# Norms 2 and 3 by token sums, eight plain block products for the first feed-forward pair, and the last down group by token halves

## Chip, core and metric

The kernel runs on one core of one Trainium2 chip. The metric is the device time of one execution in microseconds (us); the kernel before takes 1563.1 us (median of 3 runs, 1559.49 to 1563.49).

## What is computed

One encoder block on x of 1024 tokens by 1024 features, float32. The parts that the change touches, cut from the reference:

```python
def rms_norm(x, g):
    xf = x.astype(jnp.float32)
    y = xf * lax.rsqrt(jnp.mean(xf * xf, axis=-1, keepdims=True) + NORM_EPS)
    return (y * g.astype(jnp.float32)).astype(x.dtype)
...
        x = x + jnp.concatenate([o_rwkv, o_att], axis=-1) @ w_out[l]
        h = rms_norm(x, ln2_g[l])                                        # norm 2
        gate = depthwise_conv_centred(h @ ffn_w_gate[l], ffn_conv_w[l], ffn_conv_b[l])
        x = x + (jax.nn.gelu(gate, approximate=False) * (h @ ffn_w_up[l])) @ ffn_w_down[l]
    return rms_norm(x, lnf_g)                                            # norm 3
```

h is 1024 x 1024, the gate and up weights 1024 x 2816, the down weights 2816 x 1024.

## The kernel before

Everything is kept transposed: features on the 128 partitions in 8 tiles (k = 0 to 7), tokens on the free axis. Precise products are made of three matmuls in a faster float32 format, high x high, high x low and low x high; for this each operand is split: ScalarE copies the high part (names with `hi`), VectorE or GpSimd subtracts it for the low part (`lo`). A semaphore counts each such step.

A norm before (`norm`, L603 to 605; `norm_root`, L908; `rstd`, L1340; `normalised`, L1346) runs so: ScalarE squares each finished tile of x, VectorE adds the squares into `acc` [128 x 1024]; TensorE multiplies `acc` by a matrix of ones, which gives the sum of every token on all 128 partitions; ScalarE takes the root of [128 x 1024]; VectorE takes the reciprocal of [128 x 1024] into `rs`; eight products x * gain * `rs` follow. Norm 2 stands between the output projection and the feed-forward part, norm 3 ends the program.

The gate and up weights are taken in 22 pairs of column tiles (f = 0 to 21). For a pair, [gate; up] times the 2 x 2 blocks of h (B11, B12, B21, B22: feature half, token half) is made with seven block products instead of eight (`PRODUCTS`, `pair_products`, L857): operands `op` 0 to 6 are B11, t1 = B12 - B11, t2 = B22 - t1, B21, B22 - B12, B22 and B21 - t2 (x_sum, L1625, splits by `operand_hi` and `operand_lo`); weight sums are made on GpSimd (`weight_sums`, L1297 to 1302). One block product is 12 matmuls of 512 columns. Each product waits for its operand (`h_lo`), for its weights (`w_lo`), and some for an eviction of an earlier bank (`v_out`, `comb`). Pairs 0 and 1 run first, since their operands are being made meanwhile; the other 20 run in a loop. Beside pair f, ScalarE and VectorE split the weights of pair f + 1 (`pair_hi`, `pair_lo`), combine, convolve, apply GELU and multiply; the gated result goes to DRAM.

The down projection takes the 22 tiles of the gated result in groups of 8, 8 and 6. In a group each of the 8 output tiles (m) is one unit: its weights are loaded (`load_down`), split, multiplied over all 1024 tokens, and VectorE adds the result to x. In the last group a unit is 6 x 3 x 2 = 36 matmuls; ScalarE and VectorE square and sum each finished tile, so that norm 3 starts after the last one.

All engines run their own lists in the order written; only the semaphores tie them.

## Time and profile before

| | us |
|---|---|
| median of 3 runs | 1563.1 |
| the profiled execution, its own time | 1563.26 |
| its span | 1561.4 |
| output projection ends, norm 2 begins | 824 |
| first gate/up product begins | 852.36 |
| pairs run without a gap from | 884.60 |
| last matmul of the down projection ends | 1533.4 |

Of the page, these lines matter first (engine, busy us, share of the span, instructions; then forty slices of the span, with the granted TensorE clock in tenths):

```profile
PE 1411.1 (90%) x10892; PEld 1036.2 (66%) x10892; DVE 882.8 (57%) x1095; ACT 567.3 (36%) x812; POOL 182.2 (12%) x146
...
PE   6889898979899899987893699999999998999993
...
PEclk9999999989989999898996899999999999999997
```

PE is TensorE's matmuls and PEld its weight loads, DVE is VectorE, ACT is ScalarE, POOL is GpSimd, SP issues the DMAs. Each digit is a slice of 39 us. TensorE is the busiest engine and is close to full in slices 24 to 39; it is low in slices 22 and 23 (norm 2 and the first pair) and in the last one (norm 3 and the stores).

### The profile page before, as it was taken

The numbers are of one execution on the slowest core, as the hardware profiler recorded it, in microseconds if no ns is written. First come the engines' busy times: TensorE is split into PE (matmuls) and PEld (weight loads), VectorE is DVE, ScalarE is ACT, GpSimd is POOL, SyncE is SP. The second block draws the span as 40 slices with busy tenths as digits, with TensorE's granted clock in tenths as the row PEclk, the third lists the DMA queues.
The fourth block names the chain that finished last, engine by engine and source line by source line (L and its number), as shares of the span: only waits on it lengthen the run. The fifth ranks groups of instructions, "written<-read, shape, count | busy, mean of one in ns | idle before, by whom it ended". The sixth has DMA issues, their size and how long they took to land. (4 is left out here: it accounts for less than half of the span.)

```text
span 1561.4 us, 27687 instructions
## 1 busy us (share of the span) xinstructions
PE 1411.1 (90%) x10892; PEld 1036.2 (66%) x10892; DVE 882.8 (57%) x1095; ACT 567.3 (36%) x812; POOL 182.2 (12%) x146
## 2 busy tenths in 40 slices
PE   6889898979899899987893699999999998999993
PEld 3354545454477687765782588888888887888882
DVE  5664563759456567675437855555555563332235
ACT  3424141411146566666212544333334442121121
POOL 0110000101001000003034022222222200000000
PEclk9999999989989999898996899999999999999997
DMA  5036557385636657541141022222222236322112
GB/s 201 31 87 146 121 125 168 83 181 153 171 113 220 202 159 234 162 136 58 41 161 41 18 88 87 89 82 81 81 81 81 81 137 253 107 81 91 40 30 107
DMA packets 168439, 179.86 MB, mean 115 GB/s; under 512 B 76784, under 2 KB 132208, under 8 KB 168272
## 3 DMA queue, kind: packets, MB, share of 16 engines
q1 hardware_dynamic: 158800, 163.22, 35.3%
q0 software_dynamic: 2880, 9.83, 2.0%
q10 hardware_dynamic: 6720, 6.29, 1.3%
q8 instruction: 23, 0.38, 0.1%
q14 instruction: 16, 0.13, 0.0%
HBM read 121.76 MB, written 57.54 MB: 115 GB/s over the span
## 5 line engine op out<-in xcount | busy, mean ns | idle before, releaser
L872 PE MATMUL banks<-op,sw_hi 128*128 128x512 f32 x1232 | 381.8, 391 | 32.8 <-DVE op L1327 30.4
L872 PEld LDWEIGHTS banks<-op,sw_hi 128*128 128x128 f32 x1232 | 232.6, 189 | 83.5 <-issue 35.4
L576 PE MATMUL banks<-hT,work 128*128 128x512 f32 x576 | 255.1, 603 | 18.3 <-DVE hT L1386 6.4
L872 PE MATMUL banks<-op,sw_lo 128*128 128x512 f32 x616 | 240.6, 391 | 0.0
L576 PEld LDWEIGHTS banks<-hT,work 128*128 128x128 f32 x576 | 110.5, 193 | 159.9 <-issue 146.6
L1608 DVE TENSOR_TENSOR xT<-xT,banks 128x1024 f32<-128x1024 f32 x32 | 39.1, 1221 | 210.7 <-PE banks L588 199.1
L872 PEld LDWEIGHTS banks<-op,sw_lo 128*128 128x128 f32 x616 | 116.3, 189 | 24.3
L1124 ACT ACTIVATE sw_hi<-work 128x1024 fp32r<-128x1024 f32 (+1 forms) x66 | 78.9, 1200 | 96.1 <-PE banks L872 94.7
L588 PE MATMUL banks<-g_hi,down_hi 128*128 128x512 f32 x352 | 109.5, 392 | 4.0 <-DVE g_lo L1327 4.0
L1327 DVE TENSOR_TENSOR sw_lo<-work,sw_hi 128x1024 fp32r<-128x1024 f32 (+1 forms) x63 | 88.0, 1398 | 39.8 <-ACT sw_hi L1124 39.7
L588 PE MATMUL banks<-g_lo,down_hi 128*128 128x512 f32 x352 | 109.2, 392 | 0.0
L588 PE MATMUL banks<-g_hi,down_lo 128*128 128x512 f32 x352 | 109.0, 391 | 0.0
L1086 ACT ACTIVATE down_hi<-work 128x1024 fp32r<-128x1024 f32 (+1 forms) x24 | 23.6, 988 | 176.4 <-PE banks L588 176.4
L588 PEld LDWEIGHTS banks<-g_hi,down_hi 128*128 128x128 f32 x352 | 66.5, 189 | 18.2 <-DVE g_lo L1327 4.4
L588 PEld LDWEIGHTS banks<-g_lo,down_hi 128*128 128x128 f32 x352 | 66.6, 189 | 14.0
L588 PEld LDWEIGHTS banks<-g_hi,down_lo 128*128 128x128 f32 x352 | 66.6, 189 | 13.9
L1297 POOL TENSOR_TENSOR work<-work 128x512 f32<-128x512 f32 x22 | 29.0, 1317 | 346.1 <-DMA work<-in_w_gu 346.1
L1164 ACT ACTIVATE hT<-banks,par 128x1024 f32<-128x1024 f32 x22 | 24.6, 1118 | 115.8 <-DVE banks L1662 115.8
L1397 DVE SCALAR_TENSOR_TENSOR work<-banks,par,work 128x1023 f32<-128x1023 f32 x12 | 15.4, 1280 | 82.4 <-ACT work L932 82.4
L745 PE MATMUL banks<-work 32*64 32x64 f32 x1024 | 40.0, 232 | 15.1 <-DMA work<-TI_d 5.1
L745 PEld LDWEIGHTS banks<-work 32*64 32x64 f32 x1024 | 35.4, 143 | 20.3 <-ACT work L1074 9.9
L588 PE MATMUL banks<-h_hi,w_hi 128*128 128x512 f32 x128 | 41.0, 402 | 6.1 <-DVE h_lo L1327 3.0
(187 smaller groups left out, 2184.7 us busy)
## 6 DMA issues: line engine op xcount, KB each, us to landing
work<-scan_d SPq DMA_DIRECT2D x32, 768.0 KB, 4.9
work<-in_w_gu SPq DMA_DIRECT2D x88, 256.0 KB, 4.0
scan_d<-work SPq DMA_DIRECT2D x16, 1024.0 KB, 6.0
g_d<-hT SPq DMA_DIRECT2D x22, 512.0 KB, 3.0
work<-in_w_in SPq DMA_DIRECT2D x20, 512.0 KB, 3.8
scan_d<-work SPq DMA_DIRECT2D x32, 256.0 KB, 6.2
work<-in_w_down SPq DMA_DIRECT2D x16, 512.0 KB, 3.9
work<-g_d SPq DMA_DIRECT2D x15, 512.0 KB, 4.6
```

Source lines behind the costliest of these rows:

```text
L576: mm = pe.matmul(out[:, h * HALF:(h + 1) * HALF], wt[:, k, :], src[:, k, h * HALF:(h + 1) * HALF], start=(k == 0), stop=(k == kn - 1))
L588: mm = pe.matmul(out[:, h * HALF:(h + 1) * HALF], wp[slot][:, k, :], xp[k][:, h * HALF:(h + 1) * HALF], start=(opens and k == (ks or range ...
L745: pe.matmul(XY[z][64 * e:64 * e + 64, j * HD:(j + 1) * HD], Gs[slot][hk, z, j, c2 * 64:c2 * 64 + 64], UV[slot][hk, z, c2, j, :], start=(j ...
L872: mm = pe.matmul(banks[:, 3 * slot + bank, :], w[:, n, k * P:(k + 1) * P], x[n][:, k, :], start=(opens and k == 0 and p_ == 0), stop=(k == ...
L1086: act.activation(dst[slot][:, 0:kn, :], raw[slot][:, 0:kn], ACT.Copy).then_inc(wt["hi"][slot], 1)
L1124: act.activation(sw_hi[:, lo_:hi_, :], wsrc[slot][:, lo_:hi_], ACT.Copy).then_inc(fs["w_hi"], 1)
L1164: act.activation(ga[slot], flat[:, 3 * slot * HALF:(3 * slot + 2) * HALF], ACT.Copy, scale=col("cw1", f))\
L1297: pool.tensor_tensor(x[:, 1], x[:, 7], x[:, 6], ALU.add).then_inc(fs["sums"], 1)
L1327: tt(out, x, hi.bitcast(F32), ALU.subtract).then_inc(done, 1)
L1397: stt(dst[:, 1:T], ps[slot][:, 0:T - 1], col("mu_prev", m), dst[:, 1:T], ALU.mult, ALU.add)\
L1608: tt(x, x, product, ALU.add).then_inc(added[slot], 1)
```

## The change

Norms 2 and 3 in compact form: `token_norm` makes the sum of each token with one column of ones, so that tokens stand on partitions and the sums of 1024 tokens are [128 x 8]; root and reciprocal act on that; `spread` multiplies a broadcast column by the identity, which puts the values back on all partitions as [128 x 1024] in PSUM (`rms_rows`), where `normalised` reads them.

The first pair: the eight plain block products (4 weight blocks x 2 token halves), whose operands need no sums; its 4 weight blocks are split in [128 x 512] pieces by ScalarE and VectorE. The operand sums and the remaining splits move behind its start, pair 1 stays with seven products but waits for each operand by `H_NEEDED`, and the steps of pair 0 (convolution, GELU, gating) are written out between them. GpSimd no longer makes sums or low parts for pair 0, and starts the sums of pair 2 once all operands are split.

The last down group: all 8 output tiles for tokens 0 to 511, then all 8 for tokens 512 to 1023. The 8 tiles' weights are loaded in the first half and kept for the second. In the second half norm 3 of the first half's tokens runs, with its two TensorE steps behind units 1 and 2, and its 8 outputs are stored (SP); after the last unit the norm of the other half follows.

The diff, cut to its core:

```diff
-H_FIRST = 3
+PLAIN = ((0, 0, 0), (1, 0, 2), (0, 1, 1), (1, 1, 6), (2, 2, 0), (2, 3, 1), (3, 2, 2), (3, 3, 6))
+H_NEEDED = (3, 7, 8, 5, 9, 6, 10)
...
+            def token_norm(count, ts_=range(NT)):
+
+                pe.wait_ge(ns["summed"], count)
+                for t in ts_:
+                    mm = pe.matmul(token_sums[:, t:t + 1], acc[:, t * P:(t + 1) * P], ones[:, 0:1], start=True, stop=True)
+                mm.then_inc(ns["ms_mm"], 1)
+            def spread(n, ts_=range(NT)):
+
+                pe.wait_ge(ns["rstd"], n + 1)
+                for t in ts_:
+                    mm = pe.matmul(rms_rows[:, t * P:(t + 1) * P], token_rms[:, t:t + 1].broadcast_to([P, P]), ident[:, :],
+                                   start=True, stop=True)
+                mm.then_inc(ns["ms_mm"], 1)
...
-            norm(1, acc)
+            token_norm(2 * (KD - 1))
+            spread(1)
+            def eight_products():
+
+                x_at = (0, 4, 3, 5)
+                for n, (w_at, x, bank) in enumerate(PLAIN):
+                    if n in (0, 1, 4):
+                        pe.wait_ge(fs["w_lo"], (1, 2, 0, 0, 3)[n])
+                    if n in (0, 2, 4, 5):
+                        pe.wait_ge(sp_s["h_lo"], (3, 0, 4, 0, 5, 6)[n])
+                    for k in range(4):
+                        for p_, (w, x_) in enumerate(((sw_hi, op_hi), (sw_hi, op_lo), (sw_lo, op_hi))):
+                            mm = pe.matmul(banks[:, bank, :], w[:, w_at, k * P:(k + 1) * P], x_[x_at[x]][:, k, :],
+                                           start=(n < 4 and k == 0 and p_ == 0), stop=(k == 3 and p_ == 2),
+                                           skip_group_check=True)
+                    if n % 2:
+                        mm.then_inc(fs["prod"], 4 if n == 7 else 1)
...
-                    if first and slot == 0:
-                        pe.wait_ge(sp_s["h_lo"], H_FIRST + n)
+                    if first:
+                        pe.wait_ge(sp_s["h_lo"], H_NEEDED[n])
...
+            eight_products()
+            pair_products(1, 1, True)
+            pe.wait_ge(fs["x_sums"], 7)
...
+            f0, fn = GROUPS[-1]
+            n0 = down_unit(len(GROUPS) - 1)
+            for h in range(2):
+                for m in range(KD):
+                    i, slot = m // 2, m % 2
+                    if h == 0:
+                        pe.wait_ge(wt["lo"][slot], n0 + i + 1 + FREE)
+                    pe.wait_ge(added[slot], n0 + 4 * h + max(i - 1, -h) + FREE)
+                    for k in range(fn):
+                        if h == 0 and m == 0:
+                            pe.wait_ge(fs["g_lo"], f0 + k + 1)
+                        g = g_place(f0 + k)
+                        for p_, (w, x) in enumerate(((last_hi, g_hi), (last_hi, g_lo), (last_lo, g_hi))):
+                            mm = pe.matmul(banks[:, 6 * slot + i % 2, :], w[m][:, k, :], x[g][:, token_half[h]],
+                                           start=(k == 0 and p_ == 0), stop=(k == fn - 1 and p_ == 2))
+                    mm.then_inc(wt["used"][slot], 1)
+                    if h == 1 and m == 1:
+                        token_norm(3 * (KD - 1), range(4))
+                    if h == 1 and m == 2:
+                        spread(2, range(4))
+            token_norm(4 * (KD - 1), range(4, NT))
+            spread(3, range(4, NT))
...
+            def norm_root(n, ts_=slice(0, NT)):
+
+                act.wait_ge(ns["ms_mm"], 2 * n if n else 1)
+                out, sums = (token_rms[:, ts_], token_sums[:, ts_]) if n else (rs, ps[2])
+                act.activation(out, sums, ACT.Sqrt, bias=eps[:, 0:1], scale=1.0 / D).then_inc(ns["root"], 1)
...
+            act.wait_ge(src_full[0], 64)
+            for w_at, b in ((0, 0), (1, 7), (2, 3), (3, 6)):
+                w = act.activation(sw_hi[:, w_at, :], wsrc[0][:, b], ACT.Copy)
+                if w_at != 2:
+                    w.then_inc(fs["w_hi"], 1)
             norm_root(1)
...
             operand_hi(0, B11)
+            operand_hi(4, B12)
+            act.wait_ge(ns["scaled"], 2 * KD)
+            operand_hi(3, B21)
+            act.wait_ge(s["out_stored"], 16 * KD)
+            operand_hi(5, B22)
+            pair_hi(1, 1, 0)
             act.wait_ge(fs["x_sums"], 1)
             operand_hi(1, t1)
             act.wait_ge(fs["x_sums"], 2)
-            act.wait_ge(sp_s["h_lo"], 4)
+            act.wait_ge(sp_s["h_lo"], 7)
             operand_hi(2, t2)
-            act.wait_ge(ns["scaled"], 2 * KD)
-            operand_hi(3, B21)
-            act.wait_ge(fs["prod"], 1)
-            act.activation(V, banks[:, 0, :], ACT.Copy).then_inc(fs["v_out"], 1)
             act.wait_ge(fs["x_sums"], 3)
-            operand_hi(4, B12)
-            act.wait_ge(s["out_stored"], 16 * KD)
-            operand_hi(5, B22)
-            act.wait_ge(fs["x_sums"], 4)
-            operand_hi(6, B21)
+            act.wait_ge(fs["prod"], 3)
+            act.activation(ga[0], ps[0], ACT.Copy, scale=col("cw1", 0)).then_inc(fs["scaled"], 1)
+            pair_hi(1, 1, 1)
+            operand_hi(4, B22)
...
+            act.sem_inc(fs["v_out"], 1)
+            act.wait_ge(fs["prod"], NPROD + 1)
+            act.activation(V, banks[:, 3, :], ACT.Copy).then_inc(fs["v_out"], 1)
+            pair_hi(1, 1, 2)
+            act.wait_ge(fs["x_sums"], 5)
+            act.activation(ga[0], ga[0], ACT.Gelu, bias=col("cb", 0)).then_inc(fs["gelu"], 1)
+            act.wait_ge(fs["x_sums"], 6)
+            operand_hi(6, B21)
...
+            def last_weights_hi(m):
+
+                if m >= 2:
+                    for slot in range(2):
+                        act.wait_ge(wt["used"][slot], down_unit(len(GROUPS) - 1) + FREE)
+                act.wait_ge(wt["full"][m % 2], 16 * (down_unit(len(GROUPS) - 1) + m // 2) + 16)
+                act.activation(last_hi[m][:, 0:LAST_N, :], down_raw[m % 2][:, 0:LAST_N], ACT.Copy).then_inc(wt["hi"][m % 2], 1)
+
+            def square_half(h, k):
+
+                act.wait_ge(added[k % 2], down_unit(len(GROUPS) - 1) + KD // 2 * h + k // 2 + 1 + FREE)
+                if k >= 3:
+                    act.wait_ge(ns["summed"], (2 + h) * (KD - 1) + k - 2)
+                out = acc if k == 0 else sqb[k % 2]
+                act.activation(out[:, token_half[h]], xT[:, k, token_half[h]], ACT.Square).then_inc(ns["squared"], 1)
...
+            norm_root(2, slice(0, 4))
+            for k in range(KD):
+                square_half(1, k)
+            norm_root(3, slice(4, NT))
...
-            for slot in range(2):
-                weight_sums(slot, slot, 64)
-            for g, (lo_, hi_) in enumerate(((0, 2), (2, 4), (4, 7))):
-                pool.wait_ge(fs["w_hi"], g + 1)
-                pool.tensor_tensor(sw_lo[:, lo_:hi_, :], wsrc[0][:, lo_:hi_], sw_hi[:, lo_:hi_, :].bitcast(F32), ALU.subtract)\
-                    .then_inc(fs["w_lo"], 1)
+            weight_sums(1, 1, 64)
+            pool.wait_ge(sp_s["h_lo"], 10)
...
+            def rstd(n, ts_=slice(0, NT)):
 
                 dve.wait_ge(ns["root"], n + 1)
-                dve.reciprocal(rs, rs).then_inc(ns["rstd"], 1)
-                dve.wait_ge(ns["rstd"], n + 1)
+                dve.reciprocal(token_rms[:, ts_], token_rms[:, ts_]).then_inc(ns["rstd"], 1)
+                dve.wait_ge(ns["ms_mm"], 2 * n + 1)
...
-                    stt(hT[:, k, :], xT[:, k, :], col(gain, k), rs, ALU.mult, ALU.mult).then_inc(ns["scaled"], 1)
+                    stt(hT[:, k, :], xT[:, k, :], col(gain, k), rms_rows, ALU.mult, ALU.mult).then_inc(ns["scaled"], 1)
...
+            for w_at, b in ((0, 0), (1, 7), (2, 3), (3, 6)):
+                dve.wait_ge(fs["w_hi"], (1, 2, 3, 3)[w_at])
+                w = tt(sw_lo[:, w_at, :], wsrc[0][:, b], sw_hi[:, w_at, :].bitcast(F32), ALU.subtract)
+                if w_at != 2:
+                    w.then_inc(fs["w_lo"], 1)
+            dve.sem_inc(fs["comb"], 8)
...
             normalised("ln2", range(4))
             dve.wait_ge(ns["scaled"], KD + 4)
-            x_sum(t1, B12, B11)
-            operand_lo(0, B11)
-            dve.wait_ge(fs["x_sums"], 1)
-            operand_lo(1, t1)
+            operand_lo(0, B11, 1)
+            operand_lo(4, B12, 2)
             normalised("ln2", range(4, KD))
             dve.wait_ge(ns["scaled"], 2 * KD)
+            operand_lo(3, B21, 3)
+            operand_lo(5, B22, 4)
+            x_sum(t1, B12, B11)
+            dve.wait_ge(fs["x_sums"], 1)
+            dve.wait_ge(fs["prod"], 2)
             x_sum(t2, B22, t1)
-            x_sum(B12, B22, B12)
             dve.wait_ge(fs["x_sums"], 2)
-            operand_lo(2, t2)
-            operand_lo(3, B21)
+            dve.wait_ge(sp_s["h_lo"], 6)
+            x_sum(B22, B22, B12)
...
-            dve.wait_ge(sp_s["h_lo"], 6)
+            pair_lo(1, 1, 0)
+            operand_lo(1, t1, 5)
+            operand_lo(2, t2, 6)
+            pair_lo(1, 1, 1)
+            dve.wait_ge(fs["scaled"], 1)
+            g, gate = ga[0], ps[0]
+            stt(g[:, 1:T], gate[:, 0:T - 1], col("cw0", 0), g[:, 1:T], ALU.mult, ALU.add).then_inc(fs["x_sums"], 1)
+            dve.wait_ge(fs["x_sums"], 4)
+            stt(g[:, 0:T - 1], gate[:, 1:T], col("cw2", 0), g[:, 0:T - 1], ALU.mult, ALU.add).then_inc(fs["x_sums"], 1)
+            early_sum(1, 1, 0)
+            dve.wait_ge(sp_s["h_lo"], 8)
             x_sum(B21, B21, t2)
-            early_sums(0, 0)
-            dve.wait_ge(fs["x_sums"], 4)
-            operand_lo(4, B12)
-            operand_lo(5, B22)
-            operand_lo(6, B21)
-            dve.wait_ge(fs["w_lo"], 3)
-            dve.wait_ge(sp_s["h_lo"], H_FIRST + NPROD - 1)
-            pair_lo(1, 1, 0)
-            rest_of_pair(0, 0)
-            early_sums(1, 1)
+            dve.wait_ge(fs["x_sums"], 6)
+            operand_lo(4, B22, 7)
+            pair_lo(1, 1, 2)
+            early_sum(1, 1, 1)
+            operand_lo(6, B21, 8)
+            dve.wait_ge(fs["gelu"], 1)
+            for h, bank in enumerate((2, 6)):
+                dve.wait_ge(fs["prod"], NPROD)
+                half = ga[0][:, h * HALF:(h + 1) * HALF]
+                gated_half = tt(half, half, banks[:, bank, :], ALU.mult)
+            gated_half.then_inc(fs["x_sums"], 1)
+            dve.wait_ge(sp_s["h_lo"], 10)
             pair_lo(2, 0, 0)
...
+            for m in range(KD):
+                add_half(0, m)
+                if m < KD - 2:
+                    low_part(last_lo[m + 2][:, 0:LAST_N, :], down_raw[m % 2][:, 0:LAST_N], last_hi[m + 2][:, 0:LAST_N, :],
+                             wt["hi"][m % 2], down_unit(len(GROUPS) - 1) + m // 2 + 2, wt["lo"][m % 2])
+                if m >= 2:
+                    add_square_half(0, m - 1)
+            add_square_half(0, KD - 1)
+            for m in range(KD):
+                add_half(1, m)
+                if m >= 2:
+                    add_square_half(1, m - 1)
+                if m == 2:
+                    rstd(2, slice(0, 4))
+                if m >= 3:
+                    normalised_half(0, range(2 * m - 6, 2 * m - 4) if m < 7 else ())
+            add_square_half(1, KD - 1)
+            rstd(3, slice(4, NT))
+            normalised_half(1, range(KD))
```

## Rows read from the trace of the kernel before

**Rows 1.** Stages: stretch, its us, each engine's busy us (instructions), clock, DMA.
```profile
824.00:852.00 28.00, 3.87 (x6) 1.18 (x4) 22.59 (x10) 9.25 (x7) 11.75 (x5) 0.63 0.16 56
852.00:887.00 35.00, 22.47 (x83) 17.51 (x84) 32.90 (x20) 14.12 (x10) 6.87 (x3) 0.81 0.00 1
1468.00:1534.00 66.00, 65.40 (x289) 53.83 (x287) 22.09 (x21) 13.36 (x14) 0.00 (x0) 1.00 0.11 30
1534.00:1561.40 27.40, 2.98 (x4) 0.82 (x4) 19.23 (x12) 3.45 (x3) 0.00 (x0) 0.57 0.39 153
```

**Rows 2.** Chain of waits in time: start us, us, what ran.
```profile
884.60 402.84 PE banks L872 x1776
```

**Rows 3.** TensorE timeline, norm 2 to pair 1: start, us, [idle before].
```profile
828.10 3.64 PE L599 MATMUL banks<-bonusT,ones 128*128 128x512 f32 x4 [3.87 <-DVE bonusT L1338]
...
852.36 1.19 PE L872 MATMUL banks<-op,sw_hi 128*128 128x512 f32 x2 [20.62 <-DVE op L1327]
...
869.22 1.19 PE L872 MATMUL banks<-op,sw_hi 128*128 128x512 f32 x2 [9.74 <-DVE op L1327]
...
877.10 0.47 PE L872 MATMUL banks<-op,sw_hi 128*128 128x512 f32 x1 [0.66 <-issue]
```

**Rows 4.** VectorE timeline, same stretch.
```profile
825.40 2.55 DVE L1338 TENSOR_TENSOR bonusT<-bonusT 128x1024 f32<-128x1024 f32 x2
...
832.92 6.55 DVE L1343 RECIPROCAL bonusT<-bonusT 128x1024 f32<-128x1024 f32 x1 [4.97 <-ACT bonusT L911]
...
839.51 3.51 DVE L1349 SCALAR_TENSOR_TENSOR hT<-xT,par,bonusT 128x1024 f32<-128x1024 f32 x1
...
848.85 3.36 DVE L1327 TENSOR_TENSOR op<-hT,op 128x2048 fp32r<-128x2048 f32 x1
...
866.79 2.29 DVE L1327 TENSOR_TENSOR op<-bonusT,op 128x2048 fp32r<-128x2048 f32 x1
```

**Rows 5.** ScalarE and GpSimd timelines, same stretch.
```profile
831.78 1.11 ACT L911 ACTIVATE bonusT<-banks,c_eps 128x1024 f32<-128x1024 f32 x1 [5.20 <-PE banks L599]
...
846.64 1.91 ACT L1133 ACTIVATE op<-hT 128x2048 fp32r<-128x2048 f32 x1 [10.49 <-DVE hT L1349]
...
850.14 3.20 POOL L1299 TENSOR_TENSOR work<-work 128x512 f32<-128x512 f32 x1
```

**Rows 6.** Groups by shape: line, operation xcount | busy us, mean ns.
```profile
L1124 ACT ACTIVATE sw_hi<-work 128x1024 fp32r<-128x1024 f32 x44 | 46.3, 1056 | 81.1 <-PE banks L872 81.0
...
L1327 DVE TENSOR_TENSOR sw_lo<-work,sw_hi 128x1024 fp32r<-128x1024 f32 x42 | 51.3, 1223 | 39.8 <-ACT sw_hi L1124 39.7
...
L1650 DVE TENSOR_TENSOR hT<-hT,banks 128x512 f32<-128x512 f32 x44 | 30.0, 684 | 19.8 <-PE banks L872 19.8
...
L1297 POOL TENSOR_TENSOR work<-work 128x512 f32<-128x512 f32 x22 | 29.0, 1317 | 346.1 <-DMA work<-in_w_gu 346.1
...
L1006 ACT ACTIVATE work<-work,c_eps 128x8 f32<-128x8 f32 x8 | 2.0, 292 | 0.0
...
L1513 DVE RECIPROCAL work<-work 128x4 f32<-128x4 f32 x16 | 2.9, 178 | 0.6
```

**Rows 7.** TensorE timeline: eight 128-column float32 operations, and two gaps.
```profile
736.77 1.03 PE L827 MATMUL banks<-ident,hT 128*128 128x128 f32 x8
...
744.19 0.74 PE L588 MATMUL banks<-h_hi,w_hi 128*128 128x512 f32 x2 [1.40 <-POOL h_lo L1290]
...
1300.92 1.22 PE L588 MATMUL banks<-g_hi,down_hi 128*128 128x512 f32 x2 [3.98 <-DVE g_lo L1327]
```

**Rows 8.** VectorE timeline of the tail, after the last matmul.
```profile
1533.44 1.22 DVE L1608 TENSOR_TENSOR xT<-xT,banks 128x1024 f32<-128x1024 f32 x1 [5.80 <-PE banks L588]
...
1541.43 6.55 DVE L1343 RECIPROCAL bonusT<-bonusT 128x1024 f32<-128x1024 f32 x1 [4.31 <-ACT bonusT L911]
...
1548.02 9.66 DVE L1349 SCALAR_TENSOR_TENSOR hT<-xT,par,bonusT 128x1024 f32<-128x1024 f32 x8
```

**Rows 9.** DMA issues: x count, KB each, us to landing.
```profile
work<-in_w_down SPq DMA_DIRECT2D x8, 384.0 KB, 3.1
```

143 lines of the change are left out of this document (83 added, 60 removed).

## Prediction

> **What bounds the kernel now.** I read the stages first [rows 1]. Between 907 and 1290 us and in the down projection TensorE has no gap: the chain of waits has 1776 matmuls in one piece of 402.84 us [rows 2], 0.2268 us each, so a block product of 12 costs 2.72 us and one of the last group's units of 36 costs 8.16 us. No part of the change shortens that. What is left is in three places. From 824 to 852 us TensorE is busy 3.87 of 28.00 us; from 852 to 887 it is busy 22.47 of 35.00 us; from 1534 to the end it is busy 2.98 of 27.40 us [rows 1]. In the TensorE timeline the reader is to see who ends the gaps [rows 3]: norm 2's sum starts at 828.10, the first product at 852.36 when VectorE has split B11, then come gaps of 9.74 us (again a VectorE split) and 0.66 us; the piece of rows 2 starts at 884.60, with the seventh product of pair 0. Pair 1 so ends at 884.60 + 8 x 2.72 = 906.4 us. VectorE is the limit in both norm stretches (32.90 of 35.00 us busy [rows 1]), and one half of its load is plain size: a reciprocal of 6.55 us, sums and splits of 2048 elements at 2.29 us, 2.21 start to start [rows 4].
>
> All sums below are against the profiled execution, 1563.26 us (span 1561.4 and 1.9 around it); it lies 0.16 us above the median, so I take its number as the median's.
>
> **Part 1, norm 2.** Unchanged up to the last add of squares, which ends at 827.95 [rows 4]. Before, 11.56 us pass until the first normalised tile starts at 839.51 [rows 4]: sum 3.64 [rows 3], root 1.11 [rows 5], reciprocal 6.55 and handovers. After: `token_norm` is 8 float32 matmuls of one column. Nothing like it stands in the trace. The nearest row is eight 128-column operations, 1.03 us in all, and since the last lasts 0.27, 0.109 us start to start at the full clock [rows 7]. A float32 matmul is two records (rows 3 has 4 for the two of the old sum), so 16 records: 1.7 us at 2.4 GHz, 3.4 at 1.2 GHz. TensorE has idled 3.87 us before it, and the old sum took 0.85 us a record there, with a mean granted clock of 0.63 in the stretch [rows 1, 3]; I take 3.4, and 0.35 for start and drain. The root on [128 x 8] is 0.29, the reciprocal of [128 x 4] 0.18 [rows 6], for 8 columns 0.2, each with 0.05 for the handover. `spread` is 8 matmuls of 128 columns, again 16 records: 1.7 or 3.4 us; 3.4 and 0.2, as nothing dense ran before it. Sum 7.9, less the bounds 4.5 (both at full clock) and 11 (0.3 a record). So normalising starts at 835.6 instead of 839.5: gain 3.9. Cover: the 4 + 4 weight pieces put ahead of root and reciprocal are 4 x 0.6 on ScalarE (half of 1.06 and a start; behind its last square, which the add at 827.95 has waited for) and 4 x 0.61 on VectorE (0.68 less the overlap; 827.95 to 830.5) [rows 4, 6], both before the token sums end at 831.7; without that cover they would cost 2.4.
>
> **Part 2, normalising and pairs 0 and 1.** Take 835.6 as zero. The rows show a price that goes away: the first normalising instruction took 3.51 us while GpSimd made low parts, and the split of B11 3.36 instead of 2.29 while it made sums [rows 4, 5]; undisturbed the eight of norm 3 take 9.66 / 8 = 1.2 [rows 8]. GpSimd now has nothing to do here. The SBUF page of the Trainium skill (SBUF — State Buffer, Who interferes with whom) says that only a VectorE instruction with two SBUF inputs contends with GpSimd, and normalising now reads one of them from PSUM; by that rule it would be free of the price even with GpSimd busy, by the rows it is free because GpSimd is idle, and the sum is the same.
>
> VectorE: four tiles to 4.8; ScalarE's high part of B11 (1.91 [rows 5]) to 6.8; low part to 9.1. TensorE starts at 9.2, that is 844.8 instead of 852.36. Eight products are 96 x 0.2268 = 21.8 us. The restart at the lower clock costs what it did before: products 0 and 1 ran from 852.36 to 859.48, 1.5 us over 24 x 0.2268 [rows 3]; I take 1.6. They end at 32.6 if the operands keep up, and they do: low part of B12 at 11.3 (needed 16.3), B21 at 20.4 (needed 21.7), B22 at 22.6 (needed 24.4). The 9.74 us gap is gone; 12 matmuls more (2.7 us) are its price.
>
> Then VectorE's list, at 2.21 a step, is t1 24.8, t2 27.2, B22 - B12 29.5, pair 1's first weights 30.6 (1.15 [rows 6]), low t1 32.9; ScalarE makes the high part of t2 only behind that (34.8), low t2 37.2, second weights 38.3. Pair 1's products 0 and 1 fill 32.6 to 38.0, product 2 waits 0.4, product 3 ends at 43.9. VectorE goes on with two convolution steps (40.9), Q (41.6), B21 - t2 (43.8), low part of B22 - B12 (46.1), third weights (1536 elements, 1.7: 47.8) and U2 (48.4). Product 4 needs all of these: **a new gap of 4.6 us**, and with it 1.6 for the clock, since behind 3.98 us of idling two matmuls took 1.22 us and behind 1.40 us two took 0.74 [rows 7]. Products 4 to 6 end at 58.3. Pair 1 ends at 835.6 + 58.3 = 893.9 instead of 906.4: parts 1 and 2 gain **12.5 us**. GpSimd starts pair 2's sums when the last operand is split (50.7), two are there at 53.3, high and low parts at 55.6, 2.7 before TensorE asks. (Sums are 1.3 each [rows 6].) From there on the loop is the old one.
>
> **Part 3, the last group.** Twice 8 units of 18 matmuls: as many as before. In the first half weights come twice as fast, one set of 384 KB in 4.08 us, landing after 3.1 us [rows 9]. A unit's raw buffer is free 1.9 us after the unit two earlier ends, +3.1 for the load, high part 0.85, and the low part, behind VectorE's next add, is there 2.2 us before its unit. In all, a load may be 4.5 us late before TensorE waits; I charge nothing. Per unit VectorE has 0.68 + 0.95 + 0.68 and ScalarE 0.85 + 0.6 of 4.08 (0.95 and 0.85 are halfway between the times for 512 and 1024 columns [rows 6]).
>
> In the second half two steps stand in TensorE's stream. Token sums of 4 columns: 8 records, 0.9. `spread` behind unit 2 waits for the reciprocal, which VectorE's list has behind the add of unit 2 itself (0.2 + 0.68), a square's add (0.6) and 0.18: TensorE idles 1.8 us, too little for the clock [rows 7], then 0.9. Cost **3.6 us** (bounds 1.8, the wait hidden, and 5.5).
>
> After the last matmul, before: 1561.4 - 1533.4 = 28.0, of which 9.66 normalising, 6.55 reciprocal, 3.7 from the last tile to the end [rows 8]. After: add 0.7, square 0.65, add 0.7 (512 columns, [rows 6]), token sums of 4 columns 1.2, root 0.3, reciprocal 0.2, spread 0.9 to 1.8 and 0.3 around it, eight half tiles at 0.67 (1.2 less 512 / 1024 of 1.07) 5.4, stores 3.7: 14.6. Gain 13.4, net **9.8**.
>
> Code: the last group's 288 matmuls are now written out instead of looped. The page Runtime: NRT & Kernel Launch (Instruction fetch mechanics) of the Trainium skill says that sequential fetch is hidden and taken branches may stall; by it the written-out code costs 0. The straight code of pair 0 has one gap of 0.66 us that no semaphore explains [rows 3]. Three more of those would be 2 us; zero is in the sum, 2 in the range.
>
> **Sum.** 1563.3 - 12.5 - 9.8 = **1541.0 us**. Own range 1535.5 to 1546.5: norm 2 -3.4 to +3.1, the clock behind the new gap 0 to 2.3, part 3 -1.8 to +1.9, code +2, not all at one end.
>
> **Rivals.**
> (a) GpSimd's late start becomes the new wait. Against VectorE splits its sums took 3.20 us instead of 1.3 [rows 5], VectorE 3.36 for 2.29. If all four do, the second pair of sums is ready at 61.4 instead of 55.9, pair 2's first weights at 59 and its second at 64: TensorE loses 1 to 2, and VectorE's late work runs into pair 2's evictions for as much again. With a norm 2 at its long bound: 1546.5 to 1552. For it: nothing hides the sums but 2.7 us. Against: VectorE's gating reads PSUM.
> (b) Small matmuls and the spread run at full clock, the clock holds through the new gap: 1531 to 1535.5.
> (c) The halves bring nothing: unit by unit the weights come 1 us late (5 units) and the two inserted steps cost 8. The tail gains about 1: 1548 to 1553.
> (d) Slower: the weight supply of the first half decides. The point is a landing of 7.6 us (3.1 + 4.5); beyond it each of the 6 late units waits for the excess. To end above 1568 it must eat 22 + 5 us, 4.5 a unit, a landing of 12 us: 1568 to 1580. For it: the load rate doubles to 96 GB/s and every load is asked for only when its buffer is free. Against: the DMA share is 0.11 in that stretch [rows 1], 0.22 when doubled.
> (e) It doesn't do what it says: the compact root and reciprocal cost as much as the big ones, by handovers, and the operands keep VectorE as late as before: within 5 us of 1563.
>
> **Chances.** Forecast 0.68, (b) 0.10, (a) 0.11, (c) 0.04, (d) 0.04, (e) 0.03. The range 1534 to 1549 takes in the forecast, half of (b) and most of (a). About 0.3% (4.7 us) is what a measurement of this kernel can tell from no change. Faster by more: 0.93; within: 0.03; slower: 0.04.
>
> **What the profile after would show.** First gate/up product near 845, eight products without a gap, one gap of 4 to 5 us before pair 1's fifth product, ended by VectorE's U2 (L1650 before), then one piece to the down projection. GpSimd silent all through norm 2 and pair 0, until about 886. In the last half-group one idle of 1.8 us behind the third unit, and 14 to 15 us from the last matmul to the end. The forecast is wrong if a float32 matmul of one column costs over 0.6 us, if TensorE waits for `last_lo` weights, or if pair 2 starts with a wait for GpSimd's sums.

## The result, and the profile after

| | before | after |
|---|---|---|
| median of the runs made together | 1561.3 us (1557.5 to 1563.49) | 1543.5 us (1541.41 to 1550.63) |
| ratio of the times, 95% interval | 1 | 0.9889 [0.9844, 0.9933] |
| profiled execution (its span) | 1563.26 us (1561.4) | 1550.63 us (1548.8) |
| mean granted TensorE clock | 0.953 | 0.955 |

The change makes the kernel 1.1% faster, some 17.8 us, where 22.3 were forecast; 1543.5 lies within 1534 to 1549. One later execution of the kernel before took 2931.81 us, nearly twice as long as all others, and stands in no ratio. The profiled execution of after is the longest of its four and only 12.6 us below that of before, so the first reading is where the difference of the two spans lies. The stages, chosen to answer rows 1 (columns as there: stretch, its us, busy us of TensorE, its weight loads, VectorE, ScalarE, GpSimd, then the granted clock and the DMA share):

```profile
830.80:852.00 21.20, 7.56 (x34) 6.97 (x32) 13.28 (x14) 7.11 (x8) 0.00 (x0) 0.58 0.21 75
852.00:903.00 51.00, 45.64 (x180) 36.83 (x181) 42.95 (x29) 21.82 (x16) 8.66 (x6) 0.91 0.09 31
1470.00:1534.50 64.50, 63.03 (x285) 51.85 (x283) 27.97 (x42) 14.53 (x22) 0.00 (x0) 1.00 0.18 59
1534.50:1548.80 14.30, 3.55 (x17) 3.12 (x16) 7.52 (x12) 0.89 (x2) 0.00 (x0) 0.60 0.41 152
```

Counted from an event that both kernels have, the end of norm 2's last add of squares (827.95 before [rows 4], 834.76 after):

| stretch, us | before | after | difference |
|---|---|---|---|
| start to the last add of squares (code unchanged) | 828.0 | 834.8 | +6.8 |
| to the first normalised tile | 11.56 | 8.10 | -3.5 |
| from there to the first block product | 12.85 | 9.34 | -3.5 |
| from there to the end of pair 1 | 54.1 | 50.9 | -3.2 |
| to the last matmul of the down projection | 627.0 | 631.5 | +4.5 |
| to the end | 28.0 | 14.3 | -13.8 |

The first line isn't the change's. Between these two executions 6.4 of the 6.8 us arise from 455 to 525 us, in the first steps of the scan; over the profiles below the same event lies anywhere from 825.2 to 835.8 us, in kernels whose code is the same up to there. Without it the profiled execution would be 1543.8. The lines under it are steady to some tenths from one profile to the next, so the parts are sized by them, and the whole by the medians.

TensorE after, in the two stretches (start us, us, tiles, count, [idle before and what ended it]):

```profile
834.91 3.54 PE L632 MATMUL banks<-ones,bonusT 128*128 128x1 f32 x16 [3.87 <-DVE bonusT L1441]
...
839.04 3.78 PE L639 MATMUL banks<-ident,work 128*128 128x128 f32 x16 [0.59 <-DVE work L1446]
...
852.20 1.20 PE L900 MATMUL banks<-op,sw_hi 128*128 128x512 f32 x2 [9.38 <-DVE op L1430]
...
891.29 0.70 PE L921 MATMUL banks<-op,sw_hi 128*128 128x512 f32 x2 [3.48 <-DVE hT L1761]
...
900.30 0.70 PE L921 MATMUL banks<-op,sw_hi 128*128 128x512 f32 x2 [1.69 <-DVE hT L1772]
```

VectorE, then GpSimd, in the same time:

```profile
838.79 0.20 DVE L1446 RECIPROCAL work<-work 128x8 f32<-128x8 f32 x1 [1.62 <-ACT work L982]
...
842.86 4.86 DVE L1452 SCALAR_TENSOR_TENSOR hT<-xT,par,banks 128x1024 f32<-128x1024 f32 x4 [3.88 <-PE banks L639]
...
890.46 0.68 DVE L1761 TENSOR_TENSOR hT<-hT,banks 128x512 f32<-128x512 f32 x1
...
896.07 3.48 DVE L1430 TENSOR_TENSOR sw_lo<-work,sw_hi 128x1024 fp32r<-128x1024 f32 x2 [1.53 <-ACT sw_hi L1201]
...
899.48 0.67 DVE L1772 TENSOR_TENSOR hT<-hT,banks 128x512 f32<-128x512 f32 x1
```

```profile
893.59 1.28 POOL L1404 TENSOR_TENSOR work<-work 128x512 f32<-128x512 f32 x1 [86.63 <-DVE op L1430]
...
896.20 2.27 POOL L1407 TENSOR_TENSOR work<-work 128x512 f32<-128x512 f32 x1
```

Most of the forecast signs are there. The sums of norm 2 are 16 records of one column and take 3.54 us, its reciprocal 0.20 instead of 6.55 [rows 4]. The first product is at 852.20, 9.34 us behind the first normalised tile, since the four tiles take 4.86 us and none of them 3.51 [rows 4]. There is no gap for 35.6 us, then one of 3.48 us, ended by U2 (L1761); product 4 of pair 1 starts 48.43 us from the first tile. GpSimd is silent for 86.63 us. The last row of the TensorE fence was not forecast: 1.69 us before pair 1's last product, ended by `up_second` (L1772). The two splits ahead of that add (896.07) take 3.48 us beside GpSimd's sums of 2.27 us; in the kernel before two such splits met no sums and took 2.36:

```profile
881.49 2.36 DVE L1327 TENSOR_TENSOR sw_lo<-work,sw_hi 128x1024 fp32r<-128x1024 f32 x2
```

So 1.1 of these 1.69 us are again VectorE and GpSimd meeting. From pair 1's last product on the chain of waits has one piece, as before [rows 2]:

```profile
900.30 383.80 PE banks L921 x1692
```

The last group's second half and the tail (TensorE, then VectorE):

```profile
1506.28 0.95 PE L632 MATMUL banks<-ones,bonusT 128*128 128x1 f32 x8
...
1512.94 1.16 PE L639 MATMUL banks<-ident,work 128*128 128x128 f32 x8 [1.47 <-DVE work L1446]
...
1536.72 1.43 PE L632 MATMUL banks<-ones,bonusT 128*128 128x1 f32 x8 [2.18 <-DVE bonusT L1893]
...
1538.71 2.08 PE L639 MATMUL banks<-ident,work 128*128 128x128 f32 x8 [0.56 <-DVE work L1446]
```

```profile
1538.48 0.18 DVE L1446 RECIPROCAL work<-work 128x4 f32<-128x4 f32 x1 [1.81 <-ACT work L982]
...
1540.83 5.36 DVE L1899 SCALAR_TENSOR_TENSOR hT<-xT,par,banks 128x512 f32<-128x512 f32 x8 [2.17 <-PE banks L639]
```

Sums (0.95 us) and spread (1.16 us, behind 1.47 us of idle time) stand in the second half's stream; unit 1 to unit 2 takes 5.03 us and unit 2 to unit 3 6.82, where the others take 4.08: 3.7 us in all, at full clock (the stretch to 1534.5 has 1.00). Behind the last matmul the reciprocal of 6.55 us is one of 0.18 (rows 8 against this fence) and normalising takes 5.36 instead of 9.66. The written-out code of the 288 matmuls shows no gap but the 1.47 us in front of the spread. By the page Runtime: NRT & Kernel Launch (Instruction fetch mechanics) of the Trainium skill, sequential fetch is hidden; the trace agrees (no such gap in the 69 us from 1465.6 to 1534.5).

### The profile page after: what moved, and what is told of

Its sections match the earlier page's. It is cut to its first block, busy times and chain, and to the rows that moved or that the text cites. A ratio compares the mean times of both kernels' runs of the same rounds, so it can differ in the third digit from the quotient of the medians.

```text
span 1548.8 us, 27771 instructions
## 1 busy us (share of the span) xinstructions
PE 1426.1 (92%) x10960; PEld 1053.1 (68%) x10960; DVE 866.4 (56%) x1120; ACT 544.0 (35%) x803; POOL 164.7 (11%) x139
## 4 chain that ended last, share of the span: by engine, by line
PE 76%; DVE 10%; ACT 5%; DMA 4%; issue 3%; POOL 1%; SPq 1%; ACTq 1%; DVEq 0%; POOLq 0%
PE banks L921 25%; PE banks L593 17%; PE banks L605 15%; PE banks L956 4%; PE banks L777 2%; PE banks L787 2%; PE banks L806 2%; PE banks L616 2%; ACT work L1093 2%; PE banks L758 1%; PE banks L747 1%; PE banks L694 1%; PE banks L821 1%; PE banks L737 1%; DVE op L1430 1%
## 5 line engine op out<-in xcount | busy, mean ns | idle before, releaser
L921 PE MATMUL banks<-op,sw_hi 128*128 128x512 f32 x1176 | 363.8, 391 | 5.2 <-DVE hT L1761 3.5
L921 PEld LDWEIGHTS banks<-op,sw_hi 128*128 128x128 f32 x1176 | 221.3, 188 | 52.0 <-DVE sw_lo L1430 3.9
L921 PE MATMUL banks<-op,sw_lo 128*128 128x512 f32 x588 | 229.5, 390 | 0.0
L1711 DVE TENSOR_TENSOR xT<-xT,banks 128x1024 f32<-128x1024 f32 x24 | 29.3, 1221 | 169.1 <-PE banks L605 157.1
L1430 DVE TENSOR_TENSOR sw_lo<-work,sw_hi 128x1024 fp32r<-128x1024 f32 (+1 forms) x63 | 89.1, 1414 | 39.3 <-ACT sw_hi L1201 39.3
L605 PE MATMUL banks<-g_hi,down_hi 128*128 128x512 f32 x256 | 79.8, 393 | 5.4 <-DVE g_lo L1430 4.8
L605 PE MATMUL banks<-g_lo,down_hi 128*128 128x512 f32 x256 | 79.3, 391 | 0.0
L605 PE MATMUL banks<-g_hi,down_lo 128*128 128x512 f32 x256 | 79.3, 391 | 0.0
L605 PEld LDWEIGHTS banks<-g_hi,down_hi 128*128 128x128 f32 x256 | 48.5, 190 | 16.0 <-DVE g_lo L1430 5.2
L605 PEld LDWEIGHTS banks<-g_lo,down_hi 128*128 128x128 f32 x256 | 48.5, 189 | 10.2
L605 PEld LDWEIGHTS banks<-g_hi,down_lo 128*128 128x128 f32 x256 | 48.4, 189 | 10.0
```

What stands on the lines that cost most here:

```text
L605: mm = pe.matmul(out[:, h * HALF:(h + 1) * HALF], wp[slot][:, k, :], xp[k][:, h * HALF:(h + 1) * HALF], start=(opens and k == (ks or range ...
L921: mm = pe.matmul(banks[:, 3 * slot + bank, :], w[:, n, k * P:(k + 1) * P], x[n][:, k, :], start=(opens and k == 0 and p_ == 0), stop=(k == ...
L1430: tt(out, x, hi.bitcast(F32), ALU.subtract).then_inc(done, 1)
L1711: tt(x, x, product, ALU.add).then_inc(added[slot], 1)
```

## The experiments

For the single parts one source was made in which norms, eight products and halves each have a switch; with all three on it is meant to do what the kernel after does, which has a source of its own. Times are medians beside runs of the kernel before on the same chip (19 runs, 1564.4 us, for the first four below; 1561.4 for the other four). The ratio, taken over the runs, and not the difference of the medians says what a change is worth; the two differ by up to 2.2 us. All stage figures stand in one table behind the experiments.

### The kernel after, again

No edit: the kernel after, beside its parts.

> The changed kernel again, beside the three parts alone. Theory A (the first profile of it ran 6.8 us late before the change's first instruction): its stages are as before, 8.1 us from the last add of squares to the first normalised tile, 60.2 from there to the end of pair 1, 14.3 from the last matmul to the end, and its time is 17 to 21 us below the kernel before. Rival: the late upstream part belongs to the change, and is there again; then it stands 10 to 14 us below.

1548.6 us, ratio 0.9885 [0.9851, 0.9919]. This is the same ratio as in the first comparison (0.9889), at a time 5 us higher, as the kernel before is 3 us higher too. The change is worth 1.1%, 18 us by the ratio (the medians differ by 15.8). In this profile the first gap is 4.26 us and the second 0.54, and pair 1 ends at 60.15 us from the first tile, as at 60.2 above: pair 1's last product starts at 57.43 us (57.44 above) whatever the clock does between the two gaps, since VectorE's list releases it.

### Halves alone

```diff
-NORM2, EIGHT, TAIL = True, True, True
+NORM2, EIGHT, TAIL = False, False, True
```

> The kernel before with part 3 alone (last down group and norm 3 by token halves). Theory A: the parts add, each is worth what its own stage shows: 13.7 us less behind the last matmul, 3.7 us more inside the group, so 10 us less in all (1553 against 1563). Rival (the halves bring nothing because the rest of the chain hides them, or starve for weights): within 2 us of the kernel before, with waits of TensorE on the weights' low parts.

1554.1 us, ratio 0.9935 [0.9903, 0.9967]: 10.2 us of gain (5 to 15 in the interval), where 9.8 were forecast. The tail is 13.23 us instead of 28.04, and the stretch up to pair 1 is as before (78.2 us against 78.5). Part 3 stands alone and was sized right.

### Compact norms alone

Norm 2 and norm 3 (undivided) by token sums, root and reciprocal of [128 x 8] and spread; products and last group as before.

```diff
-NORM2, EIGHT, TAIL = True, True, True
+NORM2, EIGHT, TAIL = True, False, False
```

> The kernel before with both norms in compact form, the last one over all tokens at once, pairs and down group as before. Theory A: norm 2's chain from the last add of squares to the first normalised tile falls from 11.6 to 8.1 us, and behind the last matmul 3 us go (28.0 to 25): 6 to 7 us less in all, up to 2 more since normalising reads one operand from PSUM and so does not meet GpSimd's low parts (3.51 us for its first instruction should become 1.3). Rival (small matmuls and handovers eat what the root and reciprocal give): less than 2 us.

1548.9 us, ratio 0.9887 [0.9855, 0.992]: as much as all three parts together, within the intervals. Its stages show less: 9.3 us up to the end of pair 1 (69.2 against 78.5) and 3.3 in the tail (24.8 against 28.0), 12.6 in all, which the interval of the ratio (12.5 to 22.7 us) just takes in. The stages, not these four runs, size this part. The 9.3 us is more than the 3.5 us that the shorter chain explains. TensorE, VectorE and GpSimd of this kernel:

```profile
852.55 1.19 PE L938 MATMUL banks<-op,sw_hi 128*128 128x512 f32 x2 [9.57 <-DVE op L1515]
...
866.31 1.19 PE L938 MATMUL banks<-op,sw_hi 128*128 128x512 f32 x2 [5.42 <-DVE op L1515]
```

```profile
843.02 4.86 DVE L1542 SCALAR_TENSOR_TENSOR hT<-xT,par,banks 128x1024 f32<-128x1024 f32 x4 [3.88 <-PE banks L651]
...
850.12 2.28 DVE L1515 TENSOR_TENSOR op<-hT,op 128x2048 fp32r<-128x2048 f32 x1
```

```profile
839.93 8.06 POOL L1496 TENSOR_TENSOR sw_lo<-work,sw_hi 128x1024 fp32r<-128x1024 f32 x3 [29.62 <-ACT sw_hi L1235]
```

The four tiles of the kernel before, of which [rows 4] shows the first:

```profile
839.51 7.09 DVE L1349 SCALAR_TENSOR_TENSOR hT<-xT,par,bonusT 128x1024 f32<-128x1024 f32 x4
```

In the norms-only kernel GpSimd still makes low parts of the weights while VectorE normalises, the very meeting that made one normalising step 3.51 us before [rows 4]. Now four take 4.86 us, 1.2 each. What has changed is where VectorE reads the rows of reciprocal roots: `rms_rows` is PSUM, `rs` was SBUF. The gap before product 3 is 5.42 us instead of 9.74 for the same reason: the second four tiles take 4.85 (6.93 before). Not all of it is the operand's place. Of the 3.3 us by which the first product comes nearer to the first tile (9.53 against 12.85) 2.2 are the tiles, and 1.1 are the split of B11, 2.28 us instead of 3.36 [rows 4]. That split reads SBUF alone in both kernels; here GpSimd's sums, which wait for a DMA, start behind it, 10.7 us from the first tile instead of 8.7. So part 1 removes, besides the chain, the meeting that part 2 removes by silencing GpSimd.

### Eight products alone

```diff
-NORM2, EIGHT, TAIL = True, True, True
+NORM2, EIGHT, TAIL = False, True, False
```

With `EIGHT` on, the source puts norm 2's `rs` into free columns of the weights' low parts, as the products' operands take its old place:

```python
        rs1 = rs if not EIGHT else work[:, SW_AT - KD * T + 12 * BK_:SW_AT - KD * T + 14 * BK_]
```

> The kernel before with the eight block products for pair 0 alone (norms and down group as before; the inverse root of norm 2 lies in another place, because an operand needs its old one). Theory A: from the first normalised tile to the end of pair 1 it takes 60 us instead of 66.9, so 6 to 7 us less in all; gap of about 3.5 us before pair 1's fifth product and of about 1.7 before its seventh. Rival (the eight products only pay together with the short norm, since the early list of VectorE is what limits): 0 to 3 us.

1557.7 us, ratio 0.9959 [0.9929, 0.9989], 6.4 us of gain; by stages 7.0 (71.5 against 78.5).

```profile
845.19 4.87 DVE L1542 SCALAR_TENSOR_TENSOR hT<-xT,par,work 128x1024 f32<-128x1024 f32 x4
```

```profile
895.93 1.28 POOL L1481 TENSOR_TENSOR work<-work 128x512 f32<-128x512 f32 x1 [89.87 <-DVE op L1515]
```

The rows of reciprocal roots are in SBUF here, GpSimd is silent, and the four tiles take 4.87 us. For these tiles either remedy gives the whole of it.

### Norms and halves, without the eight products

```diff
-NORM2, EIGHT, TAIL = True, True, True
+NORM2, EIGHT, TAIL = True, False, True
```

> The changed kernel with part 2 undone: compact norms and the halves, but seven products for pair 0 as before. Theory B (after the norms-only run: reading the inverse roots from PSUM takes VectorE out of GpSimd's way, and that gives most of what the eight products give): pair 1 ends 61 us after the first normalised tile, 1 us later than in the changed kernel, so the time stands 18 to 19 below the kernel before. Theory A (parts add): 6.7 us above the changed kernel, 12 below the kernel before.

1545.4 us, ratio 0.9892 [0.9853, 0.9931], against 0.9885 and 0.9889 with them. Pair 1 ends 68.1 us behind the last add of squares, with the eight products 68.3 and 67.8. Its gap before product 3:

```profile
860.98 1.19 PE L938 MATMUL banks<-op,sw_hi 128*128 128x512 f32 x2 [6.16 <-DVE op L1515]
```

The eight products take this gap of 6.16 us away, together with the 2.1 of the two later gaps (0.37 and 1.77), and pay 2.72 us for 12 more matmuls, 3.48 and 1.69 for the new gaps and the clock behind them. On top of compact norms they bring between -0.2 and +0.3 us by these profiles, and 0.9 to 1.4 against the norms alone (69.2), whose code in this stretch is the same as here (68.1). What the eight products add is not clear of the 1.1 us between these two profiles of the same code.

### Rows of reciprocal roots in SBUF

Compact norms alone, but ScalarE copies `rms_rows` to SBUF and norm 2's tiles are scaled from the copy (`token_rms` moves to another tile, since the copy takes its place).

```diff
+                act.wait_ge(ns["ms_mm"], 3)
+                act.activation(rs, rms_rows, ACT.Copy).then_inc(s["kk_chain"], 1)
...
-    stt(hT[:, k, :], xT[:, k, :], col(gain, k), rms_rows, ALU.mult, ALU.mult)
+    stt(hT[:, k, :], xT[:, k, :], col(gain, k), rs if gain == "ln2" else rms_rows, ALU.mult, ALU.mult)
```

> The norms-only kernel with one step more: ScalarE copies the inverse roots of norm 2 from PSUM to SBUF (1.1 us) and normalising reads them there. Theory B (the operand's place decides whether VectorE meets GpSimd): normalising instructions beside GpSimd's low parts go back to 2 to 3.5 us each, and the first product starts 12 to 13 us after the first normalised tile instead of 9.5. Rival (the shorter norm alone took VectorE out of the way): it stays at 9.5.

This kernel ran once, so the time (1559.0 us) is not used; the stages are.

```profile
850.72 1.19 PE L938 MATMUL banks<-op,sw_hi 128*128 128x512 f32 x2 [14.10 <-DVE op L1517]
...
868.57 1.19 PE L938 MATMUL banks<-op,sw_hi 128*128 128x512 f32 x2 [10.07 <-DVE op L1517]
```

```profile
837.77 8.27 DVE L1544 SCALAR_TENSOR_TENSOR hT<-xT,par,bonusT 128x1024 f32<-128x1024 f32 x4 [5.00 <-ACT bonusT L1243]
```

```profile
833.56 9.01 POOL L1498 TENSOR_TENSOR sw_lo<-work,sw_hi 128x1024 fp32r<-128x1024 f32 x3 [30.44 <-ACT sw_hi L1235]
...
851.78 3.21 POOL L1485 TENSOR_TENSOR work<-work 128x512 f32<-128x512 f32 x1
```

With both operands in SBUF the four tiles take 8.27 us instead of 4.86 (7.09 before), and the second four 7.92 instead of 4.85. GpSimd's low parts take 9.01 instead of 8.06. The first product is at 12.95 us from the first tile instead of 9.53, and these 3.4 us are the tiles; the gap before product 3 is 10.07 us instead of 5.42. That both stand so near the kernel before (12.85 and 9.74) is partly chance: there the tiles were faster and the split of B11 slower. Norm 2's compact chain is still there (9.22 us with the copy). This shows the place of the operand as the cause of the slow tiles. The page SBUF — State Buffer (Who interferes with whom) of the Trainium skill says that a VectorE instruction with at most one SBUF input, outside its two-port modes, does not contend with GpSimd, and one with two SBUF inputs contends with a GpSimd instruction that reads SBUF. The trace agrees, and it has a price: the tiles take 1.7 times as long. GpSimd's sum of 3.21 us (1.28 in the norms-only kernel, beside tiles that read PSUM) met mostly one of VectorE's splits (3.36 us), not the tiles. The rule was weighed in the prediction and dismissed there as leading to the same sum.

### One statement earlier

VectorE's list behind pair 1's operands: `up_second` ahead of pair 2's first weights, which wait for GpSimd's sums.

```diff
+            up_second(1, 1)
             pair_lo(2, 0, 0)
-            rest_of_pair(1, 1)
+            pair_lo(2, 0, 1)
+            gate_second(1, 1)
...
```

> The changed kernel with one statement moved: pair 1's first up-sum ahead of pair 2's first weights on VectorE. If the wait before pair 1's seventh product is this sum's place behind weights that wait for GpSimd, the gap (0.5 to 1.7 us) goes and the next pair starts without a wait; if it is VectorE's load, it stays.

This kernel ran once; only this gap of TensorE is left ahead of the long piece:

```profile
890.16 0.70 PE L921 MATMUL banks<-op,sw_hi 128*128 128x512 f32 x2 [3.49 <-DVE hT L1761]
```

The gap of 1.69 us is gone, and pair 1 ends at about 58.3 us from the first tile, which is what the prediction had. The gap was the list's order: the product needed one add, and the add was queued behind weights that VectorE couldn't split yet. What the move is worth in time depends on the clock: in the kernel after's second profile only 0.54 us were idle there.

### Lists reordered

Three moves in the kernel after: the spread one unit later with normalising started behind it; VectorE's operand and U2 ahead of the two convolution steps (and ScalarE's high part of the last operand ahead of the GELU), and `up_second` ahead of the gating; GpSimd's sums released by `w_lo` instead of by the last operand.

```diff
-                    if h == 1 and m == 2:
+                    if h == 1 and m == 3:
                         spread(2, range(4))
...
-            act.wait_ge(fs["x_sums"], 5)
+            act.wait_ge(fs["x_sums"], 4)
+            operand_hi(6, B21)
...
-            pool.wait_ge(sp_s["h_lo"], 10)
+            pool.wait_ge(fs["w_lo"], 6)
...
+            early_sum(1, 1, 0)
+            dve.wait_ge(sp_s["h_lo"], 8)
+            x_sum(B21, B21, t2)
+            dve.wait_ge(fs["x_sums"], 4)
+            operand_lo(4, B22, 7)
+            pair_lo(1, 1, 2)
+            early_sum(1, 1, 1)
             dve.wait_ge(fs["scaled"], 1)
             g, gate = ga[0], ps[0]
             stt(g[:, 1:T], gate[:, 0:T - 1], col("cw0", 0), g[:, 1:T], ALU.mult, ALU.add).then_inc(fs["x_sums"], 1)
...
             operand_lo(6, B21, 8)
+            up_second(1, 1)
```

> The changed kernel with three waits moved: pair 0's two convolution steps and its GELU behind U2 in VectorE's and ScalarE's lists, pair 1's first up-sum ahead of pair 2's weights, GpSimd's sums for pair 2 released by pair 1's third weights; and the spread of the half norm one unit later. Theory (the gaps are list order, not work): the gap before pair 1's fifth product falls from 3.5 to 4.3 us to about 1.6 and the clock no longer falls behind it (1.7), the one before the seventh (0.5 to 1.7) goes, so pair 1 ends 55 us after the first normalised tile instead of 60.2; the idle of 1.5 us behind the last group's third unit goes. 6 to 7 us below the changed kernel. Rival (VectorE's sheer load sets these gaps): pair 1's end stays at 59 to 60 and only the tail gains.

1534.5 us (1529.99 to 1544.11), ratio 0.9828 [0.9787, 0.987]: 27 us below before, and by the ratios about 9 below the kernel after (0.9885 and 0.9889; the intervals overlap a little). Against the profile of after the stages are 4.1 us shorter up to the end of pair 1 (64.2 against 68.3), 3.5 from there to the last matmul and 1.2 in the tail.

```profile
880.12 0.70 PE L921 MATMUL banks<-op,sw_hi 128*128 128x512 f32 x2 [2.62 <-DVE hT L1761]
...
1283.27 0.93 PE L605 MATMUL banks<-g_hi,down_hi 128*128 128x512 f32 x2 [2.78 <-DVE g_lo L1430]
...
1500.42 1.05 PE L639 MATMUL banks<-ident,work 128*128 128x128 f32 x8
```

The first row is the only gap left from the first product to the down projection, and the last is the spread of the first half's rows, with no idle time before it. The work is the same, so what went was order and not load: the gap before product 6, the idle before the spread, and a part of the gap before product 4, of which 1.6 us and no loss of clock were expected and 2.62 with one came. Not all 8.8 us of the stages are the moves'. Pair 1 ends 3.6 us earlier from the first tile (56.6 against 60.2) and the spread's idle is 1.5: 5.1 us, where 6 to 7 were expected. Another 1.9 lie in the row at 1283.27 and one of 0.74 us behind it, waits of the down projection in code that no move touches (4.76 and 0.68 in after); over the ten profiles the first of them is anywhere from 1.84 to 5.23. The rest is norm 2's chain (0.5) and the tail (1.2), also unchanged code. Which of the moves gave what in pair 1 was not taken apart.

### The stages of all profiles

| | add of squares at | to first tile | to first product | gaps at (idle before) | pair 1 ends | tail |
|---|---|---|---|---|---|---|
| before | 827.95 | 11.56 | 12.85 | 29.7 (9.74), 37.6 (0.66), 45.1 (1.78) | 66.9 | 28.0 |
| after | 834.76 | 8.10 | 9.34 | 48.43 (3.48), 57.44 (1.69) | 60.2 | 14.3 |
| after, again | 835.76 | 7.64 | 9.34 | 48.43 (4.26), 57.43 (0.54) | 60.15 | 13.6 |
| halves | 825.19 | 11.07 | 12.85 | 29.7 (9.21), 37.8 (0.37), 45.3 (1.78) | 67.1 | 13.2 |
| norms | 834.91 | 8.11 | 9.53 | 23.3 (5.42), 31.9 (0.28), 39.3 (1.78) | 61.1 | 24.8 |
| eight | 833.87 | 11.32 | 9.35 | 48.44 (4.25), 57.44 (0.67) | 60.2 | 28.8 |
| norms, halves | 830.07 | 7.57 | 9.53 | 23.3 (6.16), 31.3 (0.37), 38.8 (1.77) | 60.5 | 14.5 |
| rows in SBUF | 828.55 | 9.22 | 12.95 | 30.8 (10.07), 38.7 (0.46), 46.2 (1.79) | 68.0 | 25.3 |
| one statement | 833.64 | 8.10 | 9.34 | 48.42 (3.49) | 58.3 | 14.4 |
| reordered | 825.68 | 7.64 | 9.34 | 46.80 (2.62) | 56.6 | 13.1 |

Columns three to six count from the event before them: "to first tile" from the add of squares, the others from the first normalised tile; the tail from the last matmul.

## Why the prediction was right, and where it was not

| step | forecast | measured |
|---|---|---|
| chain of norm 2 | 7.9 | 8.10, 7.64 |
| first tile to first product | 9.2 | 9.34 |
| low clock at the restart | 1.6 | 2.8, 2.0 |
| U2 done | 48.4 | 48.3 |
| gap before product 4 | 4.6 | 3.48, 4.26 |
| low clock behind it | 1.6 | 1.9, 3.0 |
| wait before product 6 | none | 1.69, 0.54 |
| pair 1's end | 58.3 | 60.2 |
| parts 1 and 2 | -12.5 | -10.2, -10.7 |
| inserted in the second half | 3.6 | 3.7 |
| tail | 14.6 | 14.3, 13.6 |

**Part 1** came out by its own terms: sums 3.54 (3.4 was taken), spread 3.78 (3.4), root 0.27, reciprocal 0.20. The nearest row, eight 128-column operations, had the price, and the low clock the factor of two. The bounds of 4.5 and 11 were far too wide.

**Part 2** was right on what VectorE's list allows: first product 0.1 late, U2 on time to a tenth. Two terms failed. The clock's restart was read off one stretch, 1.5 us over full speed [rows 3]; measured in the same way, after has 12 matmuls at the lower level there and loses 2.8, its repetition 8 and 2.0. The products then end about 1 us later, and the gap before U2 is as much shorter, so this cost nothing before U2. The second did cost, and it is the step that failed: the sentence "Products 4 to 6 end at 58.3" charges product 6 with its operand alone. It also overwrites a bank that `up_second` has to read first, and that add stood behind pair 2's first weights in VectorE's list, which wait for GpSimd's sums; those started when the last operand was split (893.59 us). That is rival (a), GpSimd's late start, in small and at pair 1's last product instead of pair 2's first: 1.7 us here, of which 1.1 are the two splits' meeting with the sums (3.48 us instead of 2.36). The sums themselves came when the prediction said, 50.7 us from the first tile. The second half of the rival's price, VectorE late for pair 2's evictions, did not come (one piece of 383.80 us). The run with one statement moved takes the gap away and has the forecast's 58.3, so this is shown. In the repetition the wait is 0.54 us and the low clock behind the first gap costs 3.0 instead of 1.9, so that the end is the same; with the add moved it would gain only the 0.54.

One row was misread, without effect on the sum: the gap of 0.66 us at 877.10 [rows 3], for which the prediction keeps 2 us in its range as one "that no semaphore explains". The product behind it waits for the fifth operand's low part. That is the first of VectorE's three splits from 874.71, 6.69 us for the three, so it ends at 877.0, and in the other kernels with seven products the product also starts 0.1 us behind such a split (norms alone: 874.76 and 874.87). It is an operand wait like the others.

**Part 3** was right: -13.8 in the tail and +3.7 inserted, with +0.8 more on the way to the last group (at the start of the down projection after has two waits for VectorE's splits, 4.76 and 0.68 us, where before has one of 3.98 [rows 7]; as said, that wait differs from profile to profile, so the 0.8 can't be put down to the change). Net -9.3 against -9.8; alone it measured 10.2. No unit of the first half waits for its weights, so rival (d) has nothing for it, and (c) falls with the halves alone.

**The sum.** -10.2 and -9.3 make -19.5 where -22.3 was forecast; by the medians it is 17.8, with 10 to 24 in the interval. The mechanism held. Of the 2.8 us that are missing 2.3 lie in parts 1 and 2, 1.9 of them in pair 1's end (60.2 against 58.3).

**What the sum couldn't see.** The prediction put the end of the slow meeting down to GpSimd's silence, a gain of part 2, and set the page's rule aside because it led to the same sum. For the total it does; for the parts it doesn't. The compact norms alone take 9.3 us of the stretch, the eight products alone 7.0, both 10.2 to 10.7. Both remove the same slow meeting of VectorE and GpSimd. On top of the norms the eight products are worth nothing that these runs can tell from zero, in this order of the lists. Whether they pay in the reordered lists was not tried, nor was GpSimd's earlier release by itself. Also open: why executions differ by 10 us ahead of the change.

## What to carry to other kernels

Before two edits are added up, ask of each row that gets shorter by what rule it gets shorter; if one rule serves both, the second edit has only its costs left, and a run of each alone shows it. Where a matmul reads a freshly made operand, list every semaphore that it waits for, its output bank's readers among them, and look where each of these stands in its engine's queue. Moving one add ahead of a wait took away a gap of 1.7 us, and three such moves gave 5 us that the profiles locate, more than a quarter of what the whole change did, without any work less. Where a few executions say more than the stages do, as with the norms alone (17.7 us against 12.6), size the part by the stages.

## What the hardware did that was not expected

**The clock fell behind a shorter gap than the rows had shown.** Before, it held through idling of 1.40 us [rows 7] and 1.78 us (at 884.60; the rows behind it are 0.39 us a matmul) and fell behind 3.98 [rows 7]. After, it held through 1.47 and 1.69, with 1.00 granted behind each. It fell behind 2.62 us in the reordered kernel, and at the start of the down projection behind 2.29 with norms and halves and behind 1.84 with rows in SBUF, where 1299 to 1302 us has 0.50 (that kernel had held it through 1.79 at 883.95):

```profile
1298.15 0.72 PE L617 MATMUL banks<-g_hi,down_hi 128*128 128x512 f32 x2 [1.84 <-DVE g_lo L1517]
```

The next two stretches show the low level:

```profile
852.00:858.00 6.00, 5.80 (x14) 4.63 (x15) 6.00 (x6) 0.00 (x0) 0.00 (x0) 0.50 0.00 0
```

```profile
880.00:883.00 3.00, 2.88 (x8) 2.32 (x9) 2.96 (x3) 0.47 (x1) 2.92 (x3) 0.64 0.01 3
```

The first is the restart of after at 852.20: granted 0.50, the 1.2 GHz level, with 14 matmul records where 6 us at 2.4 GHz hold 26. The second is the reordered kernel behind its gap of 2.62 us. How long the low level lasts varies between executions of the same kernel: 12 and 8 matmuls at the restart.

**Up to 128 columns a float32 matmul's price is hardly its columns.** 16 records of one column took 3.54 us and 16 of 128 columns 3.78, both with 0.50 granted, 0.22 and 0.24 us a record. At 512 columns the columns count: 4 records of the old sum took 3.64 us, 0.91 each, with 0.54 granted.

**A reciprocal's time goes by the elements per partition**: 6.55 us for 1024 [rows 4], 0.20 for 8 and 0.18 for 4. A root of [128 x 4] on ScalarE took 0.26.
